# Gates of a bidirectional RG-LRU computed on half arrays, and the root from the tanh of half the exponent

## What is computed

```python
def block_diag_linear(t, w):       # w: 16 blocks of 64x64
    y = jnp.einsum('bsnk,nkj->bsnj', t.reshape(b, s, 16, 64), w)

r = sigmoid(block_diag_linear(xc, w_a) + b_a)
i = sigmoid(block_diag_linear(xc, w_x) + b_x)
log_a = -8 * r * softplus(-lam)
a = exp(log_a)
u = sqrt(-expm1(2 * log_a)) * (i * xc)
# h[t] = a[t] * h[t-1] + u[t], forward in time and backward
lru = (h_fwd + h_bwd) * gelu(yr)
```

## Time and profile before

| | |
|---|---|
| runs | 2118.38, 2114.95 and 2117.51 us |
| median | 2117.51 us |
| span of the profiled execution | 2116.6 us (its own time is not listed apart from these) |
| PE, ACT, DVE, POOL busy over the span | 97%, 59%, 76%, 9% |
| mean granted clock of TensorE | 0.992 of full |
| `stage_lru` | from 391.0 us to 626.9 us of the span |

### The profile page before, as it was taken

One profiled execution on the slowest core, in us unless ns is written; L12 is line 12 of the kernel. 1 busy time (PEld: TensorE's weight loads), 2 busy tenths in 40 slices (PEclk: granted clock), 3 DMA queues, 4 the chain that ended last, 5 costly groups with the idle time before them and its releaser, 6 DMA issues.

```text
span 2116.6 us, 26308 instructions
## 1 busy us (share of the span) xinstructions
PE 2060.2 (97%) x10135; PEld 1697.1 (80%) x10135; DVE 1615.8 (76%) x1600; ACT 1245.0 (59%) x1165; POOL 181.1 (9%) x130
## 2 busy tenths in 40 slices
PE   6999989999999999998999999999999999999998
PEld 4777977788888888887778888888888888888886
DVE  5776756588865532555999889989988888988986
ACT  4522255377864322434567777777777777777774
POOL 3000000000000000002620011101110011101100
PEclk8999999999999999999999999999999999999999
DMA  8666120311112211237799999999999999999994
GB/s 278 182 181 174 48 61 2 80 30 46 45 45 100 85 45 45 91 120 257 292 357 394 389 389 383 390 392 389 387 380 391 383 389 384 376 392 387 385 381 153
DMA packets 246110, 512.12 MB, mean 242 GB/s; under 512 B 8044, under 2 KB 64792, under 8 KB 246040
## 3 DMA queue, kind: packets, MB, share of 16 engines
q1 hardware_dynamic: 236688, 484.84, 62.3%
q0 software_dynamic: 6752, 19.93, 3.6%
q10 hardware_dynamic: 2600, 6.38, 1.3%
HBM read 487.53 MB, written 16.78 MB: 238 GB/s over the span
## 4 chain that ended last, share of the span: by engine, by line
PE 62%; POOL 1%; DVE 1%; DMA 1%; issue 0%; ACT 0%; POOLq 0%; DVEq 0%; ACTq 0%
PE ps_gu L2527 31%; PE ps_down L2527 16%; PE ps_projected L307 5%; PE ps_projected L2108 4%; PE ps_turn L2522 2%; POOL h_lo L2486 1%; PE ps_branch L1742 1%; PE ps_projected L1767 1%; DVE third_split L2345 0%; DVE h_lo L2345 0%; DMA lru_t<-in_const 0%; PE ps_branch L2070 0%; DMA attn_t<-h_rows,slot_token 0%; PE ps_branch L2051 0%; PE ps_branch L2082 0%
## 5 line engine op out<-in xcount | busy, mean ns | idle before, releaser
L2345 DVE TENSOR_TENSOR h_lo<-tiles,h_hi 128x2048 fp32r<-128x2048 f32 x247 | 554.6, 2286 | 62.6 <-ACT h_hi L2300 60.9
L2300 ACT ACTIVATE h_hi<-tiles 128x2048 fp32r<-128x2048 f32 x252 | 468.8, 1911 | 84.0 <-PE ps_down L2527 41.1
L2345 DVE TENSOR_TENSOR third_split<-tiles,third_split 128x2048 fp32r<-128x2048 f32 x126 | 282.9, 2287 | 39.8 <-ACT third_split L2300 36.7
L2300 ACT ACTIVATE third_split<-tiles 128x2048 fp32r<-128x2048 f32 x128 | 238.1, 1911 | 41.9 <-PE ps_down L2527 24.9
L2527 PE MATMUL ps_gu<-h_hi,moe_x_hi 128*128 128x512 f32 x640 | 250.9, 392 | 2.5 <-POOL h_lo L2486 1.5
L2527 PE MATMUL ps_gu<-h_hi,moe_x_lo 128*128 128x512 f32 x640 | 249.3, 390 | 0.0
L2527 PE MATMUL ps_gu<-h_lo,moe_x_hi 128*128 128x512 f32 x640 | 249.0, 389 | 0.0
L2527 PE MATMUL ps_gu<-third_split,moe_x_hi 128*128 128x512 f32 x768 | 239.7, 393 | 0.0
L307 PE MATMUL ps_projected<-h_hi,hi_ring 128*128 128x512 f32 x480 | 187.6, 391 | 1.1 <-PEq L916 0.5
L307 PE MATMUL ps_projected<-h_hi,lo_ring 128*128 128x512 f32 x480 | 186.8, 389 | 0.0
L307 PE MATMUL ps_projected<-h_lo,hi_ring 128*128 128x512 f32 x480 | 186.8, 389 | 0.0
(11 more groups left out here) (393 smaller groups left out, 3839.6 us busy)
## 6 DMA issues: line engine op xcount, KB each, us to landing
tiles<-in_w_gate SPq DMA_DIRECT2D x64, 2048.0 KB, 11.9
tiles<-in_w_up SPq DMA_DIRECT2D x64, 2048.0 KB, 12.5
tiles<-in_w_down SPq DMA_DIRECT2D x64, 2048.0 KB, 12.2
tiles<-in_w_ada SPq DMA_DIRECT2D x24, 1024.0 KB, 8.6
tiles<-in_w_in SPq DMA_DIRECT2D x17, 1024.0 KB, 5.2
tiles<-in_w_in SPq DMA_DIRECT2D x16, 512.0 KB, 5.3
tiles<-in_w_lru_branch SPq DMA_DIRECT2D x8, 1024.0 KB, 5.1
v<-v ACTq DMA_DIRECT2D x48, 128.0 KB, 2.4
```

What stands on the lines that cost most here:

```text
L2300: nc.scalar.activation(half(w_hi(t), i), half(raw_tile(g, t), i), ACT.Copy).then_inc(hi_ready, 1)
L2345: nc.vector.tensor_tensor(half(w_lo(t), i), half(raw_tile(g, t), i), half(w_hi(t), i).bitcast(F32), ALU.subtract).then_inc(lo_ready, 1)
```

## The change

In `gates` the 128 rows of the array are used as two halves. Block 0 of the chunk is in rows 0 to 63 and block 1 in rows 64 to 127, each with a weight tile of 64 rows and 128 columns that holds both gates of that block side by side. The results of a block go to PSUM tensors of its own (`ps_blocks`), the decay gate in one half of the partitions and the input gate in the other. There are still twelve matmuls, six for each half of the array, issued in turn. Each tanh is made in two instructions of 64 partitions, because the two blocks' results of one gate lie in different tensors.

The weights take two tiles instead of four and have no zeros, so the memset goes and the splits of the weights are 128x256.

The root is computed another way: with w = tanh(-log a / 2) it is (1 + a) sqrt(w). ACT takes the square root of the tanh itself, and DVE multiplies by 1 + a after it. Square on ACT and the DVE product before the root are gone, a DVE product after the root is new, and it is waited for.

```diff
@@ stage_lru @@
-        wg = g.acc[:, :, :].rearrange("p a (w n) -> p (a w) n", n=P)
-        wg_hi, wg_lo = b.sb("wg_hi", [P, 4, P], F32R, ctx), b.sb("wg_lo", [P, 4, P], F32R, ctx)
+        wg = g.acc[:, 0, :].rearrange("p (w n) -> p w n", n=P)
+        wg_hi, wg_lo = b.sb("wg_hi", [P, 2, P], F32R, ctx), b.sb("wg_lo", [P, 2, P], F32R, ctx)
...
-        ps_ga, ps_gx = b.ps("ps_gate_a", [P, 2, HALF], ctx), b.ps("ps_gate_x", [P, 2, HALF], ctx)
+        ps_blocks = [b.ps("ps_first_block", [P, 2, HALF], ctx), b.ps("ps_second_block", [P, 2, HALF], ctx)]
+        block_rows = [slice(0, HD), slice(HD, P)]
+        DECAY, INPUT = 0, 1
+        gate_rows = lambda gate, blk: block_rows[gate ^ blk]
@@ POOL @@
-            nc.gpsimd.memset(wg[:, :, :], 0.0).then_inc(sem["zeroed"], 1)
-            pool.wait_ge(sem["zeroed"], 1)
...
-                for w, name in enumerate(("lru_w_a", "lru_w_x")):
-                    for h in range(2):
-                        dst = wg[HD * h:HD * (h + 1), w::2, HD * h:HD * (h + 1)]
+                for gate, name in ((DECAY, "lru_w_a"), (INPUT, "lru_w_x")):
+                    for blk in range(2):
+                        dst = wg[block_rows[blk], :, gate_rows(gate, blk)]
@@ ACT, direction @@
-                if j:
-                    act.wait_ge(sem["z"], 2 * j + way - 1)
-                nc.scalar.activation(recur[:, way, :], flat(ps_ga), ACT.Tanh, scale=0.5,
-                                     bias=half_bias[:, k:k + 1]).then_inc(sem[tanh], 1)
+                for blk, rows in enumerate(block_rows):
+                    nc.scalar.activation(recur[rows, way, :], flat(ps_blocks[blk])[gate_rows(DECAY, blk), :], ACT.Tanh, scale=0.5,
+                                         bias=half_bias[rows, k:k + 1]).then_inc(sem[tanh], 1)
...
+                for blk, rows in enumerate(block_rows):
+                    nc.scalar.activation(inp[rows, way, :], flat(ps_blocks[blk])[gate_rows(INPUT, blk), :], ACT.Tanh, scale=0.5,
+                                         bias=half_bias[rows, 16 + k:17 + k]).then_inc(sem[tanh], 1)
+                act.wait_ge(sem[tanh], 4 * j + 2)
...
-                link(nc.scalar.activation(root[:, way, :], recur[:, way, :], ACT.Tanh, scale=c4n[:, k:k + 1],
-                                          bias=c4n[:, k:k + 1]))
-                nc.scalar.activation(recur[:, way, :], decay[:, way, :], ACT.Square).then_inc(sem["a2"], 1)
+                nc.scalar.activation(root[:, way, :], recur[:, way, :], ACT.Tanh, scale=c2n[:, k:k + 1],
+                                     bias=c2n[:, k:k + 1]).then_inc(sem["half_tanh"], 1)
+                act.wait_ge(sem["half_tanh"], 2 * j + way + 1)
@@ ACT, roots @@
-                    act.wait_ge(sem["z"], 2 * j + way + 1)
@@ DVE @@
             def before_root(j, way, tanh):
-                dve.wait_ge(sem["a2"], 2 * j + way + 1)
-                nc.vector.scalar_tensor_tensor(out=root[:, way, :], in0=recur[:, way, :], scalar=1.0,
-                                               in1=root[:, way, :], op0=ALU.add, op1=ALU.mult).then_inc(sem["z"], 1)
-                dve.wait_ge(sem[tanh], 2 * j + 2)
+                dve.wait_ge(sem[tanh], 4 * j + 4)
...
-            def after_root(j, way, u):
+            def after_root(j, way, w, u):
                 dve.wait_ge(sem["sqrt"], 2 * j + way + 1)
+                nc.vector.scalar_tensor_tensor(out=root[:, way, :], in0=decay[:, way, :], scalar=1.0,
+                                               in1=root[:, way, :], op0=ALU.add, op1=ALU.mult).then_inc(sem[w], 1)
+                dve.wait_ge(sem[w], j + 1)
@@ PE, gates @@
-                for a, out in ((0, ps_ga), (1, ps_gx)):
-                    w = 2 * way + a
-                    for h in range(2):
-                        cols = slice(h * HALF, (h + 1) * HALF)
-                        for m, (l, r) in enumerate(((wg_hi, xc_hi), (wg_hi, xc_lo), (wg_lo, xc_hi))):
-                            last = nc.tensor.matmul(out[:, h, :], l[:, w, :], r[:, cols], start=(m == 0), stop=(m == 2))
+                for h in range(2):
+                    cols = slice(h * HALF, (h + 1) * HALF)
+                    for m, (l, r) in enumerate(((wg_hi, xc_hi), (wg_hi, xc_lo), (wg_lo, xc_hi))):
+                        for blk, rows in enumerate(block_rows):
+                            last = nc.tensor.matmul(ps_blocks[blk][:, h, :], l[rows, way, :], r[rows, cols],
+                                                    start=(m == 0), stop=(m == 2))
```

More of the change, by code:

```diff
@@ L1261, in stage_lru @@
     with ExitStack() as ctx:
-        names = ["gate_in", "wg_hi", "wg_lo", "zeroed", "xc_hi", "xc_lo", "gates_f", "gates_b",
-                 "tanh_f", "tanh_b", "a2", "z", "ix", "sqrt", "u_f", "u_b",
+        names = ["gate_in", "wg_hi", "wg_lo", "xc_hi", "xc_lo", "gates_f", "gates_b",
+                 "tanh_f", "tanh_b", "half_tanh", "ix", "sqrt", "w_f", "w_b", "u_f", "u_b",
                  "scan_f", "lru_done", "gelu_done", "lam_exp", "decay"]
@@ L1273, in stage_lru @@
         small = b.sb("small", [P, 4, 16], ctx=ctx)
-        c4, c4n, half_bias = b.sb("c4", [P, 16], ctx=ctx), b.sb("c4n", [P, 16], ctx=ctx), b.sb("hb", [P, 32], ctx=ctx)
+        c4, c2n, half_bias = b.sb("c4", [P, 16], ctx=ctx), b.sb("c2n", [P, 16], ctx=ctx), b.sb("hb", [P, 32], ctx=ctx)
         ps_x, ps_y = g.ps_proj[:, 0:2, :], g.ps_proj[:, 2:4, :]
-        ps_ga, ps_gx = b.ps("ps_gate_a", [P, 2, HALF], ctx), b.ps("ps_gate_x", [P, 2, HALF], ctx)
+        ps_blocks = [b.ps("ps_first_block", [P, 2, HALF], ctx), b.ps("ps_second_block", [P, 2, HALF], ctx)]
+        block_rows = [slice(0, HD), slice(HD, P)]
+        DECAY, INPUT = 0, 1
+        gate_rows = lambda gate, blk: block_rows[gate ^ blk]
         flat = lambda t: t[:, :, :].rearrange("p a n -> p (a n)")
@@ L1294, in _ @@
                     pool.wait_ge(sem["wg_lo"], j)
-                for w, name in enumerate(("lru_w_a", "lru_w_x")):
-                    for h in range(2):
-                        dst = wg[HD * h:HD * (h + 1), w::2, HD * h:HD * (h + 1)]
-                        src = d[name][0, :, 2 * j + h].rearrange("w k n -> k w n")
+                for gate, name in ((DECAY, "lru_w_a"), (INPUT, "lru_w_x")):
+                    for blk in range(2):
+                        dst = wg[block_rows[blk], :, gate_rows(gate, blk)]
+                        src = d[name][0, :, 2 * j + blk].rearrange("w k n -> k w n")
                         pool.dma_start(dst, src).then_inc(sem["gate_in"], 16)
@@ L1425, in _ @@
             link(nc.vector.tensor_scalar(c4[:, :], q, -4.0, None, ALU.mult))
-            link(nc.vector.tensor_scalar(c4n[:, :], q, 4.0, None, ALU.mult))
+            link(nc.vector.tensor_scalar(c2n[:, :], q, 2.0, None, ALU.mult))
             nc.vector.tensor_scalar(half_bias[:, :], par[:, B_BA:B_BA + 32], 0.5, None,
@@ L1447, in _ @@
                     lows(j + 1)
-                after_root(j, F, "u_f")
+                after_root(j, F, "w_f", "u_f")
                 h = xc[:, j % 2, :]
@@ L1452, in _ @@
                                              ALU.add).then_inc(sem["scan_f"], 1)
-                after_root(j, B, "u_b")
+                after_root(j, B, "w_b", "u_b")
                 back = inp[:, B, ::-1]
@@ L1495, in _ @@
                 if j:
-                    pe.wait_ge(sem["tanh_b"], 2 * j)
+                    pe.wait_ge(sem["tanh_b"], 4 * j)
                 gates(j, F, "gates_f")
@@ L1502, in _ @@
                     second_gate(range(0, 2))
-                pe.wait_ge(sem["tanh_f"], 2 * j + 2)
+                pe.wait_ge(sem["tanh_f"], 4 * j + 4)
                 gates(j, B, "gates_b")
```

3 lines of the change are left out of this document (removed).

## The result

The changed kernel takes 2127.5 us in the median of four runs (2126.75 to 2130.63) against 2117.6 for the kernel before, a ratio of 1.0056 with a 95% interval of 1.0043 to 1.0068. (The ratio is that of all runs; the two medians alone give 1.0047.) The forecast was slower, 2122.4 us: the sign and the range held, but the loss is 9.9 us where 4.9 were forecast, and 4.9 lies outside the interval, which reaches from 9.1 to 14.4 us. The span of the profiled execution is 2125.9 us, 9.3 over that of before.

The account below looks back on a forecast made before the run. PE was taken to bound the stage, with chain slacks of 0.65 and 1.4 us deciding. Parts -2.2 + 0 - 1.2 + 4.9 gave +1.5 us, clock falls +3.4, together +4.9: 2122.4 us, range 2116 to 2129.

Parts of the forecast that it names:

- What bounds the kernel, and what is late next: Stage bound by PE, 27.20 us a chunk; after the change PE waits for the GELU (1.5) and DVE's split (2.8).
- The pair of halves: Gates on PE: two matmuls in different halves run together, 0.227 us a pair; rival that they don't: 2128.5 us, chance 0.12.
- The change of tiling: Gates on PE: 0.09 us added for each of two changes, so a group costs 1.54 instead of 2.72 us.
- The half tanh: ACT behind each gates group: four half tanhs cost 4.03 us, 2.02 more than two whole ones.
- The clock: PE's longer waits let its clock fall to 0.50; two falls that count, +3.4 us.
- (a): From the first forward gates to the start of the second chunk: -2.2 us.
- (b): Six chunks, 419.34 to 582.57: gates save 6 x 2.36 us, waits take back 14.2, sum 0.
- (c): The last projection and forward gates: -1.2 us.
- (d): The end: "gl" 2.1 us later, a 2.3 wait before the last 24 matmuls, ACT 0.5 late: +4.9 us.
- the clock didn't hold: Rival that PE's clock holds: the sum without falls, +1.5 us, 2119.0 us; chance 0.28.
- half tanhs aren't cheaper: Rival on ACT behind each gates group: a half tanh is cheaper than a whole one, about 2112 us; chance 0.07.
- The 8% for a chain that is longer somewhere: Case not listed, a longer chain somewhere in the kernel: slower, no size given; chance 0.08.

Follow-up runs that it names:

- whole_and_early: Changed kernel with whole tanhs (gates left unsorted to their channels) and the product with 1 + a before the root: 2101.4 us against 2116.0 before, ratio 0.9929.
- halves_alone: Kernel before the change with each tanh as two instructions over 64 partitions, nothing else changed: 2137.0 us against 2116.4, ratio 1.0098.
- order_by_rows: Changed kernel with half tanhs ordered so that two in a row write the same 64 partitions: 2129.6 us against 2116.4 before, ratio 1.0064.
- whole_tanhs: Changed kernel with each tanh one instruction over 128 partitions, gates left unsorted to their channels: 2110.0 us against 2116.4 before, ratio 0.9971.

## Why the prediction was right and wrong

**What bounds the kernel, and what is late next**: right. The two slacks of 0.65 and 1.4 us decided the case, and the waits in the loop are the two that were named, of nearly the sizes named (2.6 for 2.8, 1.5 for 1.5). In the last chunk the wait for the gate's tanh came as named (1.9 for about 2), one of 2.3 for the forward tanhs came that wasn't named, and the one of 2.3 named ahead of the last 24 matmuls came as 0.5, since a fall of the clock took up the rest. Take the two chains away and PE's 25.4 us a chunk come out, as whole_and_early shows.

**The pair of halves**: right, 0.23 us. The rule of the Trainium skill (TensorE: Matmul & The Clock Gate, Part 3), that a weight load overlaps matmuls in flight only where its row group differs, would have made the pair dearer; the trace disagrees with it, with pairs at 0.23 us while every load behind the first pair's has a matmul of its own group in flight. The same section also lets a load into the background weight buffer be pulled ahead, and the prediction left that out. Read with it, the section and the trace agree, though no run here shows which buffer a load used.

**The change of tiling**: too small, 0.09 for a measured 0.20. The rows of attention showed the first step behind a change, and I didn't look at the second. That takes 0.25 from each group's gain. The waits of the loop don't hide all of it: two chunks in turn take together the split's chain and PE's own work once, forecast 29.14 + 24.84 = 53.98, measured 27.0 + 28.0 = 55.0 (without a fall). Of this 1.0, about half is PE's own work, 25.4 instead of 24.84. Three such pairs at 0.5 and three groups outside the loop at 0.25 (the last backward group is hidden behind ACT) make an estimated 2.2 us by which this step of the prediction is short.

**The half tanh**: this is the step that failed most. "Fewer partitions make none shorter: 64x1024 takes 1036 ns", "So four half tanhs cost 4.03": the row gave a duration in flight, and I took the step between starts from whole tanhs. The step is 1.14 us, each direction costs 2.54 instead of 2.02 more, and every chain through it is 0.5 longer; halves_alone shows the same step in the kernel before. By the prediction's own price for this ("each 0.1 us off a half tanh ... about 2.4 off the whole") 0.13 more is +3.1 us. The trace bears that out: 3 x 0.5 in the pairs of chunks, and in the last chunk 0.5 in ACT's late arrival and 1.0 in its chain of eight half tanhs. I had allowed for a half tanh that is cheaper and not for one that is dearer, the side on which it fell.

**The clock**: right in kind and size, two falls that count, at 1.6 us. That it was two is in part luck: of three waits of 2.6 us two were followed by a fall, and in order_by_rows, with the same waits, three were.

**The sum**: 1.5 + 3.1 (half tanhs) + 2.2 (tiling) = 6.8 without the clock, and 6.8 + 3.2 = 10.0, against 10.2 that the stage lost. With either term alone the forecast would have been nearer but still short. By its parts: (a) -2.2 forecast, -1.6 measured; (b) 0 forecast, +5.0 measured, of which the two falls are 3.2; (c) and (d) +3.7 together forecast, +6.8 measured. Two errors cancel in these parts. (b) lists seven waits, of which six stand in the loop; the seventh, for the GELU, stands in the last chunk, and there ACT, behind its late GELU, comes 2.3 us later to the forward gates instead of the 0.5 of (d). The weights of the first chunk bring the first gates 0.3 us forward, not 0.8.

**The rivals**: the clock didn't hold; the halves do run together; half tanhs aren't cheaper. (That rival's figures don't follow from its own price: the sum is zero at about 0.95 and -5.9 at 0.7, not at 0.93 and -5.5. Nothing rests on it.) The 8% for a chain that is longer somewhere was the right thought with too small a chance.

## What to carry to other kernels

Before an engine's work is cut on the bound engine, sum the chains of the others from the point where it releases them to the point where it wants them: slack in busy time (4 to 6 us here) didn't tell what would be late, slack in the chain (0.65 and 1.4) did. Take the cost of a split instruction from starts of split instructions, and a product that has all its inputs early belongs in front of the late one, which here was worth 8 to 9 us for no instruction more. If only one of two like directions has room on the second engine, change only that one.

## What the runs showed of the hardware that I had not expected

- A tanh of 64x1024 out of PSUM is in flight as long as one of 128x1024 (1.11 us), but the next one starts 1.14 us after it instead of 1.01, in each of the three arrangements of written partitions and read PSUM tensors that were run (the changed kernel, halves_alone, order_by_rows). The cause stays open.
- A change of tiling slows two matmuls, not one: 0.32 and 0.33 us instead of 0.227, on the way in and on the way out.
- Idle times of PE of 2.6 us were followed by a fall of the clock to 0.50 in two of three cases in this loop (at 447.1 and 559.7 us, not at 503.5), and those of 1.4 to 1.7 us in the loops of this and the other kernels in none. Length alone doesn't tell: in the last chunk idle times of 1.9 us were followed by one in the changed kernel and in whole_tanhs (615.0 us), while in halves_alone idle times of 2.3 and 2.9 us in the last chunk weren't. Five matmuls without use, 1.1 us, put into the idle times of 2.6 us went with a loop without a fall. The third fall of the changed kernel, in the last chunk (617.8 us), cost nothing that can be seen, since PE waits 0.5 us for DVE's last split behind it anyway.
